# Moving the start addresses of the activation tensors and of the split weights in SBUF by half of 64 bytes

## The reference

```
for i in range(2):
    ax, ac = modulate(rms_norm(hx)), modulate(rms_norm(hc))      # adaLN from c, c_ctx
    yx, yc = even_mixer(ax, ac) if i == 0 else odd_mixer(ax, ac)  # window + neighbourhood / differential attention
    hx = hx + g1 * yx;  hx = hx + g2 * relu(modulate(hx) @ w1)**2 @ w2    # 1024 -> 4096 -> 1024
    # the same for hc in block 0
x = rms_norm(hx)
```

## The kernel before

| tensors | start, modulo 64 |
|---|---|
| `X`, `raw`, `whi`, `wlo`, `wk1`, `wk2`, `RS`, `cst`, `par`, `SC`, `small` | 0 |
| `MO`, `RC` (behind the 4 bytes of `mhalf`) | 32 |
| `Hh`, `Hl`, `aring`, `SB`, `AC`, `AR`, `pick` | 32 |
| `scs`, `stp`, `Q0`, `K0`, `V0`, `BI`, `Q1`, `K1`, `V1`, `HIDh`, `HIDl` (behind the 16 bytes of `pick`) | 0 |
| all of the last two blocks: `Gh`, `Gl`, `QZ`, `KQ`, `V2`, `GT`, `QN`, `QR`, `KN`, `VA`, `KK`, `KX`, `AL`, `IX`, `PQ`, `CQh`, `CQl` | 32 |

## Time and profile before

### The profile page before, as it was taken

The page is one execution under the profiler, slowest core; times in us unless marked ns, Lnnn a source line. Parts: engine busy times, 40 slices in busy tenths (PEclk is TensorE's granted clock), DMA queues, the critical chain, the costliest instruction groups (busy, mean ns, idle before and its releaser), DMA issues.

```text
span 1352.6 us, 25050 instructions
## 1 busy us (share of the span) xinstructions
PE 1321.1 (98%) x9434; PEld 1168.0 (86%) x9434; DVE 990.8 (73%) x1734; ACT 668.6 (49%) x1358; POOL 193.9 (14%) x268
## 2 busy tenths in 40 slices
PE   7999999999999999999999999999999999999997
PEld 6786779888888888898996899999999988999967
DVE  6698778999887878978429565655665886865874
ACT  4427744631613315344238564566465566455573
POOL 0101213000000000123105600000210016020043
PEclk8999999999999999999999999999999999999999
DMA  8783134466885868834220345655475433455511
GB/s 309 274 239 120 49 110 141 156 218 216 311 309 205 286 212 292 298 112 151 94 94 1 108 146 167 205 183 171 140 267 178 140 128 104 157 167 168 170 49 47
DMA packets 67665, 233.15 MB, mean 172 GB/s; under 512 B 7280, under 2 KB 12400, under 8 KB 67312
## 3 DMA queue, kind: packets, MB, share of 16 engines
q1 hardware_dynamic: 67568, 231.84, 50.4%
HBM read 230.76 MB, written 1.05 MB: 171 GB/s over the span
## 4 chain that ended last, share of the span: by engine, by line
PE 87%; DVE 5%; ACT 2%; issue 2%; POOL 1%; DMA 1%; SPq 0%; ACTq 0%; DVEq 0%; POOLq 0%
PE ps L1710 25%; PE ps L1711 24%; PE ps L1712 24%; PE ps L1935 4%; PE ps L1964 3%; PE ps L1995 2%; DVE wlo L957 1%; DMA aring<-aall 1%; PE ps L1979 1%; DVE ps L1031 1%; ACT wk L719 1%; PE ps L1727 1%; ACT whi L599 1%; DVE ps L1233 1%; DVE small L1246 0%
## 5 line engine op out<-in xcount | busy, mean ns | idle before, releaser
L957 DVE TENSOR_TENSOR wlo<-raw,whi 128x1024 fp32r<-128x1024 f32 (+1 forms) x284 | 347.7, 1225 | 151.4 <-ACT whi L599 145.7
L599 ACT ACTIVATE whi<-raw 128x1024 fp32r<-128x1024 f32 (+1 forms) x284 | 296.4, 1044 | 267.7 <-PE ps L1712 267.1
L1710 PE MATMUL ps<-Hh,whi 128*128 128x256 f32 (+1 forms) x896 | 303.4, 339 | 3.0 <-DVE wlo L957 1.0
L1711 PE MATMUL ps<-Hl,whi 128*128 128x256 f32 (+1 forms) x896 | 300.0, 335 | 0.0
L1712 PE MATMUL ps<-Hh,wlo 128*128 128x256 f32 (+1 forms) x896 | 300.0, 335 | 0.0
L1710 PEld LDWEIGHTS ps<-Hh,whi 128*128 128x128 f32 x896 | 169.2, 189 | 25.5 <-issue 5.2
L1712 PEld LDWEIGHTS ps<-Hh,wlo 128*128 128x128 f32 x896 | 169.1, 189 | 19.1
L1711 PEld LDWEIGHTS ps<-Hl,whi 128*128 128x128 f32 x896 | 169.4, 189 | 18.3
L1710 PE MATMUL ps<-Gh,whi 128*128 128x256 f32 x624 | 176.2, 282 | 0.5 <-DVE Gl L1164 0.4
L1710 PE MATMUL ps<-HIDh,whi 128*128 128x256 f32 (+1 forms) x536 | 176.5, 329 | 0.0
L1711 PE MATMUL ps<-HIDl,whi 128*128 128x256 f32 (+1 forms) x536 | 176.3, 329 | 0.0
(11 more groups left out here) (266 smaller groups left out, 2062.9 us busy)
## 6 DMA issues: line engine op xcount, KB each, us to landing
raw<-wall SPq DMA_DIRECT2D x270, 512.0 KB, 4.0
aring<-aall SPq DMA_DIRECT2D x144, 512.0 KB, 4.6
raw<-wall SPq DMA_DIRECT2D x14, 384.0 KB, 3.1
AL<-ali SPq DMA_DIRECT2D x14, 192.0 KB, 5.3
X<-xin SPq DMA_DIRECT2D x2, 1024.0 KB, 6.6
BI<-rpb SPq DMA_DIRECT2D x4, 512.0 KB, 9.7
out<-X SPq DMA_DIRECT2D x4, 256.0 KB, 2.4
cst<-const SPq DMA_DIRECT2D x1, 960.0 KB, 8.3
```

The costliest lines, as they stand in the source:

```text
L599: act.activation(whi[:, slot, 0:n], raw[:, slot, 0:n], ACT.Copy).then_inc(sem("w_hi"), 1)
L957: dve.tensor_tensor(wlo[:, slot, 0:n], raw[:, slot, 0:n], whi[:, slot, 0:n].bitcast(F32), ALU.subtract)\
L1710: pe.matmul(o, a[0], b[0], start=first, stop=False)
L1711: pe.matmul(o, a[0], b[1], start=False, stop=False)
```

## The change

Two unused tensors of 32 bytes are put before `whi` and behind `wlo`, `mhalf` takes 64 bytes for 4, and `pick` 64 for 16 (of which the first 16 are used as before). Nothing else is changed: the instructions, their order, their shapes and their waits are the same, but for the one-time memset of `mhalf` (L1419), which writes 16 columns for 1.

```diff
--- before.py
+++ after.py
@@ -123,8 +123,10 @@
 
         X = sb("X", [P, KT, 2 * N])
         raw = sb("raw", [P, SLOTS, 1024])
+        sb("half_line", [P, 8], F32)
         whi = sb("whi", [P, SLOTS, 1024], F32R)
         wlo = sb("wlo", [P, SLOTS, 1024], F32R)
+        sb("other_half", [P, 8], F32)
         wk1 = sb("wk1", [P, 4, 512])
         wk2 = sb("wk2", [P, 4, 512])
         RS = sb("RS", [P, 512])
@@ -137,7 +139,7 @@
         small = sb("small", [P, 4, 16])
         lam = sb("lam", [P, 8])
         nsink = sb("nsink", [P, 8])
-        mhalf = sb("mhalf", [P, 1])
+        mhalf = sb("mhalf", [P, 16])
         MO = sb("MO", [P, 2, N])
         RC = sb("RC", [P, 2, N])
 
@@ -168,7 +170,7 @@
         SB = sb("SB", [P, 3, 1024], F32, b1)
         AC = sb("AC", [P, AC_END], F32, b1)
         AR = sb("AR", [P, 2, P], F32, b1)
-        pick = sb("pick", [P, 4], F32, b1)
+        pick = sb("pick", [P, 16], F32, b1)[:, 0:4]
         scs = sb("scs", [P, KT, 32], F32, b1)
         stp = sb("stp", [P, 2, KT, 3], F32, b1)
         s0 = ExitStack()
```

## The result

The changed kernel takes 1356.76 us (median of 20), the kernel before 1354.99 us in the same set of runs; the ratio is 1.0015, with a 95% interval of 1.0009 to 1.0022. One execution of each kernel took far longer than all its others (1834.76 us before, 6127.34 us after) and has no part in the ratio. So the change costs 1.2 to 3.0 us. The forecast was -4.0 us.

A forecast was written before the change was run, and what follows sets the result against it. PE was taken to bound the kernel, busy 1321.1 of 1352.6 us, mostly in `mm3` matmul steps. Terms -8.9 + 6.0 + 0 - 1.3 + 0.2 gave -4.0 us, so 1352.1 us, range 1345 to 1361.

The forecast's parts named there:

- That PE's step sets the time and that it depends on addresses: Time is the number of `mm3` matmuls times their start-to-start step, plus a few waits; the trace shows 7.6 ns by address.
- PE's lead over `wlo` at the HID switch: Where HID tiles begin, shorter H tiles could leave next to no lead: at most 0.1 us in each of 3 quarters.
- A moving operand at 0 steps at columns + 32 cycles: `mm3` matmuls: moving operand at 32 modulo 64 pays 18 cycles more at 512 columns, some 4 fewer at 256.
- (0, 32): Moving operand at 0, stationary at 32, modulo 64; at 512 columns not in the trace, taken as columns + 32 cycles.
- HID, costed at 0: HID moving, 696 matmuls at 512 and 912 at 256 columns: no change, 0 us.
- The first rival: Distance between operands decides at 512 columns: H stays at 234.3 ns, HID +5.3 us; total +10.2, 1366.3 us; chance 0.16.
- The second: Rival: distance decides at every width; HID pays +5.3 at 512, gets -1.5 at 256; +3.8, 1359.9 us; chance 0.09.
- H, G, CQ at 256 columns, +6.0 us: 3528 matmuls with H, G or CQ moving go from 118.3 to 120.0 ns: +6.0 us.
- H at 512 columns: 1176 matmuls with H moving go from 234.3 to 226.7 ns: -8.9 us.
- the small term I added: The 24 matmuls with 384 columns, between +4 and +18 cycles by interpolation: under +0.2 us.
- Value units, -1.3 us: 768 matmuls in which the weights move, 256 columns, go from 120.0 to 118.3 ns: -1.3 us.
- The rule on two read ports: PE has independent SBUF read ports for moving operand and weight loads, so the stationary remainder can't matter; sum stays -4.0 us.

The follow-up runs named there:

- The tables: Kernels with TensorE alone, computing nothing of the reference: matmul steps over start offsets of moving and stationary operand, in project and value order; no whole-kernel time.
- the +1.6 of the table: Not a run: sum in us of step differences between the traces of the changed kernel and the kernel before, by moving operand and columns.
- the first table: TensorE alone in project order, 8 x 8 start offsets in steps of 32 bytes: 226.7 to 234.3 ns at 512 columns, 113.3 to 120.2 at 256.
- the activation half: Changed kernel without the two tensors around the weights, so only `mhalf` and `pick` are padded: ratio 0.9915 of before, 1343.93 us.
- distance 0 everywhere: On the activation half, padding added to put all activation tensors at the weights' remainder modulo 256: ratio 0.9974 of before, 1351.31 us.
- the weight half: Kernel before plus only the two tensors around `whi` and `wlo`; activations as before but 64 higher: ratio 0.9934, 1346.03 us.
- -64: As a layout: H, HID, G, CQ at distance 0 where 512 columns move, -64 bytes where 256 move; against before 0.9866, 1336.44 us.
- +112: As a layout: H, HID, G, CQ at distance 0 where 512 columns move, +112 bytes where 256 move; against before 0.9834, 1331.80 us.
- +16: As a layout: H, HID, G, CQ at distance 0 where 512 columns move, +16 bytes where 256 move; against before 0.9894, 1340.65 us.

## Why the prediction was wrong, step by step

- *That PE's step sets the time and that it depends on addresses*: right. The steps of PE moved; VectorE's and ScalarE's busy times did not by more than 0.2%, as forecast. PE's lead over `wlo` at the HID switch was not put to the test, as the H tiles before it became only 1 ns a step shorter (TensorE's waits for `wlo`: 1.1 us, 1.0 before).
- *"A moving operand at 0 steps at columns + 32 cycles, whatever the stationary one's remainder is, as far as the trace has the case"*: this is the step that failed. It was drawn from three cases at 256 and 384 columns and put on 512. The tables show that it holds neither at 512 nor at 256 columns; at 512 the distance decides: (0, 32) takes 233.3 ns. H gave 1.1 us instead of 8.9, and HID, costed at 0, paid 4.6. The first rival had this place and this price (+5.3), with 0.16. The second, "the distance decides at every width", with 0.09, was right in kind, and of the rivals with an effect it was the nearest in time (+3.8 against the +1.6 of the table): it kept H, G and CQ at 256 columns where they were. I set it aside for the earlier trace rows, 120.0 ns at a distance that is 32 modulo 64. Modulo 256 it is +96, where 120.0 is the step. What that rival had wrong is the modulus.
- *H, G, CQ at 256 columns, +6.0 us*: 0.5 came, from CQ alone. The 120.0 ns of HID and of the value units was taken as the step of a moving operand at 0; it was the step of two distances, 0 and +96. H and G went from -96 to -32, both near 118.3. The differences from the forecast are +7.8 for H at 512 columns, +4.6 for HID, -5.5 for this term, -1.1 for the value units and -0.2 for the small term I added: +5.6, from -4.0 to the +1.6 of the table. The first rival's total (+10.2) was too high because it kept the same 256-column term. The measured 1356.76 us lies inside the range I gave, 1345 to 1361 us, but that is luck: the errors of +12.4 and -6.8 us among the terms partly cancel. Its base was off too: 1356.1 is the median of three runs, twenty give 1354.99.
- *Value units, -1.3 us*: right in sign, -2.4.
- *The modulus.* I folded all addresses modulo 64, because the change speaks of 64. The trace held the warning: G at 117.3 and H at 118.6 with one pair of remainders, and I named it ("something else has a part in it") and went on. The runs show what it was: -96 has two stable steps at 256 columns, near 117.3 and 118.7, in the first table and in the trace of before, where G and H both have tiles at either. What picks one stays open.
- *The rule on two read ports* (Trainium skill, TensorE: Matmul & The Clock Gate, "Step-by-step: what each phase is for") says that a weight load takes nothing from the running matmul, and I drew from it that the stationary operand's address can't matter. The first table doesn't bear that out: with the moving operand fixed at 0 and 512 columns, moving the stationary one by 32 bytes takes the step from 226.7 to 233.4 ns. The page says nothing of addresses, and whether a port or something else costs the time no run here shows. The 119.9 against 120.0 ns that I took for agreement was a coincidence of distances 0 and +96.

## What to carry to other kernels

Where float32-rounded matmuls follow one another without a wait, each with a weight load of its own, the start addresses of the moving and the stationary tile relative to each other, modulo 256 bytes, were worth up to 1.7% of this kernel's time. A table over distances, with TensorE alone, is one kernel of 1.1 ms. The forecasts drawn from it, helped by the mixed steps at -64 that the activation half had shown, came within 0.4% of the time of four layouts of the whole kernel (distance 0 everywhere, the weight half, -64 and +112), whose effects are 0.3 to 1.7%. For a fifth (+16) it left two values open, 0.979 and 0.989, and 0.9894 was measured. Where a distance has two steps, the table doesn't say which one the kernel will take. An effect that was read at one width or modulo one number isn't to be put on another without a case at that width.

## What the runs showed of the hardware that was not expected

- The step of an F32R matmul with its load depends on the distance of the two tiles modulo 256 bytes, in the three-pass order: 226.7 to 240.0 ns at 512 columns, 113.3 to 130.3 at 256, 111.5 to 111.8 (nothing) at 128, where only multiples of 32 bytes were run. The best distances differ by width: 0 at 512; -64, +16 and +112 at 256, where 0 takes 120.0.
- Some distances have two or more stable steps at 256 columns: 113.3 and 117.8 at -64, 117.3 and 118.7 at -96, 116.7 and 117.8 at +32, and three at +16 (113.3, 116.7 and 118.7). In two traces, before and the activation half, the step changed across one wait (0.46 and 0.54 us from one start to the next, for 0.12). What picks one isn't shown. In both orders of the tables the same cells of -64 and -96 have the same step, but at -64 the same addresses took either step in one run of TensorE alone, so the addresses don't settle it.
- Narrower weight loads did not make the step shorter at distance 0 and 512 columns (231.7 ns with 32 columns, 226.7 with 128), but did at 256 columns (117.8 with 32, 113.3 with 64, 120.0 with 128).
- Which accesses meet stays open. The two simple theories, a matmul's own two addresses and the load beside the stream, both failed, and no run here separates the reads of the two operands from the writes to PSUM.
